# Attention over 64 row tiles: the exponentials of a tile at the end of its own step, the difference of its maps behind the next step's first eviction

## What is computed

```python
def diff_attend(q, k, v, q_pos, k_pos, lam):
    s = jnp.einsum('bqhcd,bkhcd->bhcqk', q.astype(jnp.float32), k.astype(jnp.float32)) / math.sqrt(DIFF_HEAD_DIM)
    mask = k_pos[None, :] <= q_pos[:, None]
    s = jnp.where(mask, s, -jnp.inf)
    p = jax.nn.softmax(s, axis=-1)
    attn = p[:, :, 0] - lam * p[:, :, 1]
    return jnp.einsum('bhqk,bkhe->bqhe', attn, v.astype(jnp.float32))
...
    o = attend(q, k, v, lam)
    o = rms_norm(o, subln_w, SUBLN_EPS) * (1.0 - lam_init)
    diff_out = o.reshape(B, T, DIFF_WIDTH) * jax.nn.silu(diff_gate.astype(f32))
```

## Time and profile before

| | us |
|---|---|
| median of 3 runs | 4914.34 |
| lowest and highest run | 4902.09, 4914.79 |
| profiled execution, its time | 4913.24 |
| its span in the trace | 4911.4 |
| PE busy, share of the span | 4096.3, 83% |
| DVE busy | 2023.2, 41% |
| ACT busy | 1751.4, 36% |
| attention of layer 0, from its first scores to its last product | 1495 to 2173 |
| attention of layer 1 | 3891.5 to 4570 |

### The profile page before, as it was taken

How to read it: one execution, slowest core, us unless ns; L and a number is a source line. 1 busy time by engine, 2 the same in 40 slices (tenths; PEclk the granted TensorE clock), 3 DMA queues, 4 the chain that set the end, 5 groups by cost and what they waited for, 6 DMA issues and landing times.

```text
span 4911.4 us, 114297 instructions
## 1 busy us (share of the span) xinstructions
PE 4096.3 (83%) x49138; PEld 3564.4 (73%) x49138; DVE 2023.2 (41%) x4536; ACT 1751.4 (36%) x3584; POOL 481.6 (10%) x264
## 2 busy tenths in 40 slices
PE   3999998788887887877979999978888788788595
PEld 2999998677774555556979999967777555555495
DVE  3111111666655555552231111136666455555335
ACT  3000000666655555651110000036666555565211
POOL 1322231000000000001033222200000000000200
PEclk9999999799998999987989999979999899999697
DMA  4211121111113344343222111111111244353333
GB/s 162 78 70 74 65 77 61 39 44 37 39 45 113 127 147 133 100 146 121 84 75 76 68 74 70 57 63 38 39 44 28 80 143 122 118 164 97 115 120 131
DMA packets 227651, 427.63 MB, mean 87 GB/s; under 512 B 32162, under 2 KB 137636, under 8 KB 212900
## 3 DMA queue, kind: packets, MB, share of 16 engines
q1 hardware_dynamic: 213316, 339.18, 21.7%
q10 hardware_dynamic: 13824, 81.07, 4.1%
HBM read 304.91 MB, written 123.80 MB: 87 GB/s over the span
## 4 chain that ended last, share of the span: by engine, by line
PE 67%; DVE 12%; ACT 8%; issue 5%; SPq 4%; DMA 4%; POOL 1%; ACTq 0%; DVEq 0%
PE psum L1881 10%; PE psum L1882 10%; PE psum L1883 10%; PE psum L1352 4%; PE psum L1380 3%; PE psum L703 3%; PE psum L1526 3%; PE psum L1528 2%; PE psum L1527 2%; PE psum L1368 2%; PE psum L1123 2%; SPq L978 2%; PE psum L700 2%; SPq L979 2%; PE psum L774 1%
## 5 line engine op out<-in xcount | busy, mean ns | idle before, releaser
L1881 PE MATMUL psum<-x_hi,w_parts 128*128 128x416 f32 x2640 | 931.4, 353 | 60.5 <-POOL w_parts L1839 60.5
L1882 PE MATMUL psum<-x_lo,w_parts 128*128 128x416 f32 x2640 | 927.3, 351 | 0.0
L1883 PE MATMUL psum<-x_hi,w_parts 128*128 128x416 f32 x2640 | 926.7, 351 | 0.0
L1848 DVE TENSOR_TENSOR arena<-psum,arena 128x416 f32<-128x416 f32 x330 | 195.5, 592 | 1284.5 <-PE psum L1883 1284.3
L322 ACT ACTIVATE arena<-arena 128x256 f32<-128x256 f32 x16 | 8.2, 514 | 1543.9 <-DVE arena L446 1543.9
L1881 PEld LDWEIGHTS psum<-x_hi,w_parts 128*128 128x128 f32 x2640 | 496.8, 188 | 68.7 <-POOL w_parts L1839 64.2
L1259 DVE TENSOR_SCALAR_CACHE_REDUCE arena<-psum 128x512 f32<-128x512 f32 (+3 forms) x640 | 357.5, 607 | 358.6 <-PE psum L1352 221.9
L1883 PEld LDWEIGHTS psum<-x_hi,w_parts 128*128 128x128 f32 x2640 | 497.1, 188 | 6.5
L1882 PEld LDWEIGHTS psum<-x_lo,w_parts 128*128 128x128 f32 x2640 | 498.2, 189 | 4.4
L1380 PE MATMUL psum<-arena 128*128 128x128 f32 x2176 | 316.9, 288 | 64.0 <-ACT arena L1172 46.8
L1352 PE MATMUL psum<-arena 64*128 64x512 f32 (+3 forms) x1280 | 325.8, 613 | 40.8 <-DVE arena L1259 22.0
(11 more groups left out here) (339 smaller groups left out, 6783.8 us busy)
## 6 DMA issues: line engine op xcount, KB each, us to landing
out_proj_t<-arena ACTq DMA_DIRECT2D x66, 1040.5 KB, 4.2
arena<-in_cache_k SPq DMA_DIRECT2D x256, 256.0 KB, 2.8
arena<-in_cache_v SPq DMA_DIRECT2D x256, 256.0 KB, 3.0
arena<-in_w_in SPq DMA_DIRECT2D x66, 512.0 KB, 3.5
arena<-out_proj_t SPq DMA_DIRECT2D x32, 1024.0 KB, 6.7
arena<-out_proj_t SPq DMA_DIRECT2D x96, 257.0 KB, 3.2
m_raw<-mixed_t SPq DMA_DIRECT2D x10, 1664.0 KB, 7.2
x_res<-x_cur SPq DMA_DIRECT2D x10, 1664.0 KB, 18.1
```

Source lines behind the costliest of these rows:

```text
L1848: dve.tensor_tensor(ost[:, b % 2, 1 + g * TG:1 + (g + 1) * TG], bank[q % 8][:, 0:TG], RSTD[:, cols(g)], ALU.mult).then_inc(p_ev, 1)
L1881: pe.matmul(bank[q % 8][:, 0:TG], w_hi[:, b % 3, k, :], x_hi[:, k, cols(g)], start=(k == 0), stop=False)
L1882: pe.matmul(bank[q % 8][:, 0:TG], w_hi[:, b % 3, k, :], x_lo[:, k, cols(g)], start=False, stop=False)
L1883: mm = pe.matmul(bank[q % 8][:, 0:TG], w_lo[:, b % 3, k, :], x_hi[:, k, cols(g)], start=False, stop=(k == KT - 1))
```

## The change

Two edits, one on ACT and one on DVE; PE, POOL and SP keep their programs.

On ACT both exponentials of tile t move from places 0 and 1 of step t + 1 into step t, to places blocks(t) + 1 and blocks(t) + 2 or the last place of the step where that is earlier, behind what that place already holds. In nearly all steps both come out at the last place, so they stand right behind one another, ahead of copy_o of that step.

On DVE the difference of tile t - 1 moves from behind the maxima of tile t to behind the eviction of its block 0. Tile 63's, whose next step has no blocks, stays.

```diff
@@ attn_scalar
                 for j in range(width(t)):
-                    if j < 2 and 1 <= t <= NTILE:
-                        exp(t - 1, j)
                     if j < blocks(t - 2):
                         copy_turned(t - 2, j)
...
                     for b, k in pieces(t, j + 1):
                         beside_scalar(act, b, k)
+                    for a in range(2):
+                        if t < NTILE and j == min(blocks(t) + 1 + a, width(t) - 1):
+                            exp(t, a)
                 if t >= 2:
                     copy_o(t - 2)
@@ attn_vector
                 for j in range(blocks(t)):
                     scores_out(t, j)
+                    if j == 0 and t:
+                        combine(t - 1)
                     beside(t, j)
                 if t < NTILE:
                     maxima(t)
-                if 1 <= t <= NTILE:
+                if t == NTILE:
                     combine(t - 1)
```

## The result

The changed kernel takes 4938.62 us (median of 5 runs, 4932.45 to 4939.19), the kernel before 4913.35 (5 runs, 4902.09 to 4914.79): 1.0062 of the time before, 95% interval 1.0048 to 1.0076. It is slower by 25 us. The forecast was 4916, a change of less than 0.3%, with a range of 4886 to 4942: the time is inside the range, but the change is not the one that was forecast. The profiled executions differ by the same: spans of 4936.7 and 4911.4 us.

The account below looks back on a forecast made before the run. The prediction took PE to bound the attention stage, busy 1119.9 of 1356.5 us. Its terms summed to +1.4 us a layer, twice +2.8, on a profiled 4913.24, giving 4916.0, range 4886 to 4942.

Parts of the forecast that it names:

- the term for steps 43 to 47: End of a head: late maximum delays turned copy and page multiplication; +2.2 us net, between -1.6 and +4, once a head.
- Step 40: PE's wait for the first turned copy grows by the second exponential; +1.5 us, between 0 and +2.8, once a head.
- the root step: Steps 36 and 37, heads 1 to 3: both exponentials ahead of the root; -5.0 us, between -1 and -6.5.
- Ordinary pairs: Steps 38 and 39: small step grows, waits for difference and eviction go; -0.7 us, between 0 and -2, five a layer.
- The value step: Steps 34 and 35: exponentials ahead of the value copy; +1.0 us in heads 1 to 3, +2.1 in head 0.
- B's sign: Step 36 grows by 4 us or more, or the low clock only moves from step 37 into 35 and 36.
- B: Rival, slower: PE's small steps decide, the clock falling in their waits for copies; +31 us, 4944; chance 0.24.
- A: Rival, faster: the wait for the difference goes and no new one comes in step 46; -34 us, 4880; chance 0.26.
- C: Rival: nothing reaches the end, exponentials start only some 0.4 us sooner and page loads swallow the rest; 4913; chance 0.10.

Follow-up runs that it names:

- act_alone: The changed kernel with DVE's old order, the difference back behind the maxima, so only the ACT edit remains; 1.0007 of the time before.
- maximum_first: The changed kernel with the difference behind the maxima in step 14 of each head alone; 1.0032 of the time before.
- root_behind: The kernel before with the root and its two table loads moved behind the second exponential, instead of between the two; 0.9957 of the time before.
- root_tile: The kernel before with both exponentials early only for the tile ahead of the root (heads 1 to 3), DVE untouched; 0.9926 of the time before.
- three_tiles: root_tile with the exponentials of the tiles of steps 11 and 13 of each head early too; 0.9921 of the time before.
- tile_39: The kernel before with the exponentials early only for the tile of step 7 of each head, DVE untouched; 1.0042 of the time before.
- clock_held: The changed kernel with 14 unused transposes on PE in step 15 of a head, ahead of its wait for the sequence's exponentials; 1.0060 of the time before.

## Why the prediction was wrong

**The step that failed** is the term for steps 43 to 47, "+2.2 net": it measured +4.6 at the end of a head. The mechanism was the one described, and the turned copy came when the working said, to 0.2 us. What the term left out is the clock. The working followed one delay to the copy and let PE's work behind it keep its length; but PE now stands twice, 1.60 and 1.80 us, the clock falls (0.79 in layer 0, 0.89 in layer 1), and in head 2 of layer 0 the work from the copy to the page multiplication took 1.7 longer. Over the two stages PE was busy 26 us longer with the same matmuls, which is about the whole loss. The term's upper bound of +4 had room for most of it. At 2.4 us in 8 heads the miss is 19 us in step lengths; by the ratios, putting the maximum first gives back 15, and the two intervals leave 4 to 25.

**Step 40** measured +2.4 in the mean of heads 1 to 3, in place of +1.5. In head 2, whose rows the prediction read, it grew by 3.85, more than the upper bound of 2.8 for "the clock falls in a wait of 3.5". In heads 1 and 3 it grew by 1.4 to 1.8, close to the term, because the clock was low there before too. Over all eight heads it is +2.05, 4 us more than forecast. Head 2 was a poor sample: steps 39 and 40 run at 1.00 there, and at 0.88 and 0.81 to 0.83 in heads 1 and 3, with the same waits. Both misses are the same choice. In the root step I counted a clock that stays up as gain, and in the two steps where a wait grows I took the value without its fall.

**Ordinary pairs** came out at 0.0 in heads 1 to 3 in place of -0.7, another 4 us over six places, while steps 9 to 13 gave 5 back that were not forecast. **The value step** (+0.9 for +1.0) and **the root step** (-5.4 for -5.0) were right. Head 0 lost 7.4 and 5.4 us in the two layers where its terms made 4.4; in act_alone it was 3.7 and 3.8, so this is the end of the head again. Together: (2.5 + 1.0) x 6 heads for heads 1 to 3, and 4 for head 0, makes 25 above the forecast's +2.8, where the spans show 22.5.

**What was to show it.** PE's wait for the difference fell under 8 us: it is gone. PE waits 33 us more for L1172 and L1039 (73.4 against 40.5; 15 or more was asked). Step 36 grew by 2.3, steps 36 and 37 are 5.4 shorter, the clock over 37 and 38 is 0.91, ACT is idle before L1047: all right. A part of B's sign came as well, since step 36 ran at 0.81. Wrong were steps 46 and 47, 4.6 longer in place of 2, and DVE's wait for the exponentials, 60.6 us and not under 50. In act_alone that wait is 33.7, so the early difference itself brings DVE there too soon.

**The rivals.** A is out: the wait in step 46 came, and even with the maximum first the time is 1.0032. C is out too: its parts reach the end, -36, +40 and +27 us. B named 4944, near the 4938.6 measured, and its reason is half right. "PE's small steps decide" holds in step 40 and at the end of a head. It does not hold in the root step: step 36 ran at 0.81, yet steps 36 and 37 were 5.4 us shorter together, not the 2 that B gave them. What B shares with a rule of the Trainium skill (TensorE: Matmul & The Clock Gate, Why this matters for your kernels), that long gaps between bursts cost the full rate, the changed kernel's trace bears out in seven of the eight steps like 40: 3.53 us of waiting, and a step at 0.74 to 0.83. In the eighth, step 8 of layer 0, the same wait left 1.00. Nor did it need a long gap: 1.87 us stood in front of 0.80 to 0.83 in six heads of the kernel before.

**What stays open.** Why the same waits bring the clock down in one head and not in another. And why maximum_first, whose steps sum to 1.3 us a head less than act_alone's in the table, is 12 us slower by the ratios (3 to 22 by the intervals). The table comes from one execution each, and these two were not typical: maximum_first's profiled execution took 4911.6 us, the shortest of its runs (median 4925), and act_alone's 4917.8, near the longest of its own (median 4908). In these two executions the order is that of the table; what makes the other executions of maximum_first longer no trace shows. The row of root_behind is of the longest of its runs, too, 4908.2 with a median of 4886.9.

**A faster version.** Of all, the tile ahead of the root alone is what pays: root_tile at 0.9926, three_tiles at 0.9921 of the kernel before, which no measurement here tells apart.

## What to carry to other kernels

An edit that is applied to every step of a loop should be costed, and tried, place by place: here 6 of 128 places gained 36 us and the others lost 40, and the edit as a whole looked like nothing. Before an operation is moved ahead of others on an engine that waits for a pair of inputs, see whether another edit has already taken that wait away; then the move can only delay what it passes. Where a wait of the array's grows, price the work behind it at the half clock as well, above all where two waits come close together. And read a place's clock in every repeat of the loop before you take it into a sum: here the one head that was read was the exception.

## What the hardware showed

The granted clock of a step in which PE waits a few us, for kernels in which the waits are the same in every head, to 0.02 us. The clocks are those of heads 0 to 3 in each layer, or of heads 0 to 2 for step 15.

| step of a head, kernel | PE's waits, us | layer 0 | layer 1 |
|---|---|---|---|
| 8, before | 1.87 | 0.80, 0.83, 1.00, 0.80 | 0.80, 0.82, 1.00, 0.81 |
| 8, after | 3.53 | 1.00, 0.83, 0.75, 0.83 | 0.74, 0.83, 0.74, 0.83 |
| 8, tile_39 | 3.53 | 0.73, 0.75, 0.74, 0.72 | 0.83, 0.75, 0.74, 0.87 |
| 15, before | none | 1.00, 1.00, 1.00 | 1.00, 1.00, 1.00 |
| 15, after | 1.60 and 1.80 | 0.79, 0.79, 0.79 | 0.89, 0.89, 0.89 |
| 15, clock_held | 1.79 | 0.89, 1.00, 1.00 | 0.89, 0.89, 0.89 |
| 15, act_alone | 0.43 and 1.11 | 0.88, 1.00, 0.88 | 0.88, 1.00, 0.88 |
| 15, maximum_first | 0.42 and 1.11 | 1.00, 1.00, 1.00 | 1.00, 1.00, 1.00 |

So the length of the waits alone does not decide. One wait of 1.8 to 1.9 us can stand in a step at 0.80, and one of 3.53 in a step at 1.00. With more and longer waits the fall is more frequent and takes more of the step: the two waits of the changed kernel were followed by it in all six steps. What else decides, these runs do not show. I had taken each wait by itself, and its clock from one head.
